# Weight casts in a fixed chain of two on GpSimd's queue, GpSimd's early arithmetic moved to VectorE

## The reference

```
h = rmsnorm(x, g_pre_mix[i])
layer 0: q,k,v,gate,mq = split(h @ w_in_ret)      # 6 heads of 128, retention in chunks of 128, rotary on q and k
         r = retention(q,k,v); self = groupnorm(r) * silu(gate)
layer 1: q,k,v,f,mq = split(h @ w_in_fox)         # 12 heads of 64, causal softmax with forget gates
mem = softmax(mq @ mk / 8) @ mv                   # 256 memory tokens, mk|mv = rmsnorm(mem) @ w_mem_kv
x = x + rmsnorm(concat(self, mem) @ w_out[i], g_post_mix[i])
h = rmsnorm(x, g_pre_mlp[i]);  u = relu(h @ w_up[i])
x = x + rmsnorm((u*u) @ w_down[i], g_post_mlp[i]) # 1024 -> 4096 -> 1024
```

## Time and profile before

| | us |
|---|---|
| median of three runs | 3964.7 |
| profiled execution | 3923.8 |
| its span, slowest core (3) | 3922.3 |
| spans of the 8 cores | 3885.5 to 3922.3 |
| TensorE busy | 3362.8 (86%) |
| VectorE / ScalarE / GpSimd busy | 1903.4 / 1722.5 / 458.3 |

### The profile page before, as it was taken

How to read it: one execution, slowest core, us unless ns; L and a number is a source line. 1 busy time by engine, 2 the same in 40 slices (tenths; PEclk the granted TensorE clock), 3 DMA queues, 4 the chain that set the end, 5 groups by cost and what they waited for, 6 DMA issues and landing times.

```text
span 3922.3 us, 56104 instructions; the slowest of 8 cores (3885.5 to 3922.3 us)
## 1 busy us (share of the span) xinstructions
PE 3362.8 (86%) x16476; PEld 1521.1 (39%) x16476; DVE 1903.4 (49%) x3201; ACT 1722.5 (44%) x3117; POOL 458.3 (12%) x422
## 2 busy tenths in 40 slices
PE   0536755699998999999999999999999999999997
PEld 0312322244443444444444444444444444444443
DVE  1435430346465654536246674565556664345252
ACT  0323310244734542574863443444734443755841
POOL 0111110001001220001011221010101210010010
PEclk9768877899999999999999999999999999999999
DMA  9779797744565554434435545445465454535334
GB/s 139 134 152 154 148 181 143 150 147 147 148 193 163 169 173 158 148 120 140 142 120 178 199 135 177 149 138 165 138 183 167 149 186 145 147 121 154 108 119 129
DMA packets 198262, 593.79 MB, mean 151 GB/s; under 512 B 49024, under 2 KB 60928, under 8 KB 196224
## 3 DMA queue, kind: packets, MB, share of 16 engines
q1 hardware_dynamic: 195296, 538.03, 45.0%
q0 software_dynamic: 2672, 52.17, 10.7%
HBM read 605.48 MB, written 88.87 MB: 177 GB/s over the span
## 4 chain that ended last, share of the span: by engine, by line
PE 66%; DMA 14%; DVE 8%; issue 4%; ACT 4%; another core or an unknown queue 2%; SPq 1%; POOL 1%; DVEq 0%; ACTq 0%; POOLq 0%
PE pb L598 66%; DMA wf_s<-wbf 6%; DMA xt_s<-xT 3%; DMA vcache<-un_s 2%; DVE un_s L618 2%; DVE tb_s L621 2%; DMA wm_s<-wbf 1%; SPq L633 1%; ACT rs_s L609 1%; ACT sq_s L609 1%; DVE hb_s L621 1%; POOL xt_s L618 1%; DMA mkv_s<-memkv 1%; DVE sq_s L618 1%
## 5 line engine op out<-in xcount | busy, mean ns | idle before, releaser
L598 PE MATMUL pb<-u_s,wf_s 128*128 128x512 bf16 x4096 | 987.4, 383 | 102.8 <-DMA wf_s<-wbf 73.7
L598 PE MATMUL pb<-hb_s,wf_s 128*128 128x512 bf16 x4096 | 968.4, 385 | 102.4 <-DMA wf_s<-wbf 75.9
L598 PE MATMUL pb<-hb_s,wm_s 128*128 128x512 bf16 (+1 forms) x2240 | 599.2, 387 | 56.0 <-DMA wm_s<-wbf 26.4
L598 PEld LDWEIGHTS pb<-hb_s,wf_s 128*128 128x128 bf16 x4096 | 396.3, 99 | 590.3 <-issue 161.1
L598 PEld LDWEIGHTS pb<-u_s,wf_s 128*128 128x128 bf16 x4096 | 398.4, 98 | 564.9 <-issue 133.8
L609 ACT ACTIVATE pt_s<-pb,dcol_s 128x512 bf16<-128x512 f32 x960 | 534.1, 628 | 71.2 <-PE pb L598 64.1
L609 ACT ACTIVATE rb_s<-pb 128x512 bf16<-128x512 f32 x512 | 304.4, 595 | 532.4 <-PE pb L598 456.8
L618 DVE TENSOR_TENSOR u_s<-rb_s 128x512 bf16<-128x512 bf16 x512 | 264.1, 516 | 497.5 <-ACT rb_s L609 496.1
L609 ACT ACTIVATE sq_s<-pb 128x512 bf16<-128x512 f32 x304 | 180.7, 596 | 712.2 <-DVE hb_s L630 678.0
L598 PE MATMUL pb<-un_s 65*128 65x512 bf16 (+5 forms) x1536 | 406.5, 305 | 12.5 <-DVE rs_s L618 4.2
L630 DVE CAST hb_s<-pb 128x512 bf16<-128x512 f32 x256 | 176.8, 691 | 452.1 <-PE pb L598 451.1
(11 more groups left out here) (65 smaller groups left out, 2403.9 us busy)
## 6 DMA issues: line engine op xcount, KB each, us to landing
wf_s<-wbf SPq DMA_DIRECT2D x512, 512.0 KB, 3.9
wm_s<-wbf SPq DMA_DIRECT2D x152, 768.0 KB, 4.8
xt_s<-xT SPq DMA_DIRECT2D x176, 256.0 KB, 6.4
wbf<-wall POOLq DMA_DIRECT2D x32, 1024.0 KB, 20.4
wm_s<-wbf SPq DMA_DIRECT2D x32, 512.0 KB, 4.2
outT<-xt_s SPq DMA_DIRECT2D x64, 256.0 KB, 2.7
wbf<-wall POOLq DMA_DIRECT2D x19, 768.0 KB, 18.1
vcache<-un_s SPq DMA_DIRECT2D x64, 144.0 KB, 4.2
```

What stands on the lines that cost most here:

```text
L598: S.add("pe", lambda e: e.matmul(out, lhsT=lhsT, rhs=rhs, start=start, stop=stop, **kw), reads=reads, writes=writes, cost=c)
```

## The change

The number of casts in flight goes from a modelled three to two that the hardware enforces: each cast names the cast two places before it as something it reads, so GpSimd waits for that cast's landing before it issues; the first two places before have none, and those casts name the fifth tile of x instead. The condition on TensorE's modelled time is gone, so all casts are recorded at the start of GpSimd's list. The cast's source and destination are written as rows of 1024 numbers (4 KB in f32) where they were 128 rows. For the first two blocks of the first sequence the elementwise operations that ran on GpSimd go to VectorE (`spare`), and `fox_prep` clears its tiles there always.

```diff
-NCAST = 3
+NCAST = 2
...
+    def rows(ap, o, n):
+        return ap[o * 131072:(o + n) * 131072].rearrange("(r f) -> r f", f=1024)
...
             r_ = gR[keys[0]]
-            if i >= NCAST:
-                p_ = rs_[i - NCAST]
-                yield lambda: S.avail["pe"] >= p_.last_w.end - 3000.0
-            yield ("pool", [], [])
-            S.add("pool", (... e.dma_start(out=d_, in_=s_).then_inc(sem, 16))(flat(DR["wbf"], o, n), flat(DR["wall"], o, n)),
-                  writes=[r_], dma=True, ncast=n)
+            after = [rs_[i - NCAST]] if i >= NCAST else [X[items[0]]["x"][4].R]
+            yield ("pool", after, [])
+            S.add("pool", (... e.dma_start(out=d_, in_=s_).then_inc(sem, 16))(rows(DR["wbf"], o, n), rows(DR["wall"], o, n)),
+                  reads=after, writes=[r_], dma=True, ncast=n)
...
+    def spare(s, b):
+        return "dve" if s == 0 and b < 2 else "pool"
...
-            tt(xs[c].ap, xs[c].ap, t.ap, ALU.add, ..., eng=("pool" if c % 2 else "dve"))
+            tt(xs[c].ap, xs[c].ap, t.ap, ALU.add, ..., eng=(spare(s, b) if c % 2 else "dve"))
...
-            tt(dst.ap, t1.ap, swp.ap, ALU.add, [t1.R, swp.R], [dst.R], eng="pool")
+            tt(dst.ap, t1.ap, swp.ap, ALU.add, [t1.R, swp.R], [dst.R], eng=e_)
...
-            tt(mix[:, h, :], rs.ap, sg.ap, ALU.mult, [rs.R, sg.R], [mixR[h]], eng="pool")
+            tt(mix[:, h, :], rs.ap, sg.ap, ALU.mult, [rs.R, sg.R], [mixR[h]], eng=spare(s, b))
...
-            memset(t.ap[:, :, 1, :], 1.0, [], [t.R], eng="pool")
+            memset(t.ap[:, :, 1, :], 1.0, [], [t.R])
```

More of the change, by code:

```diff
@@ L543, in caster @@
             r_ = gR[keys[0]]
-            if i >= NCAST:
-                p_ = rs_[i - NCAST]
-                yield lambda: S.avail["pe"] >= p_.last_w.end - 3000.0
-            yield ("pool", [], [])
-            S.add("pool", (lambda d_, s_: lambda e, sem: e.dma_start(out=d_, in_=s_).then_inc(sem, 16))(flat(DR["wbf"], o, n), flat(DR["wall"], o, n)),
-                  writes=[r_], dma=True, ncast=n)
+            after = [rs_[i - NCAST]] if i >= NCAST else [X[items[0]]["x"][4].R]
+            yield ("pool", after, [])
+            S.add("pool", (lambda d_, s_: lambda e, sem: e.dma_start(out=d_, in_=s_).then_inc(sem, 16))(rows(DR["wbf"], o, n), rows(DR["wall"], o, n)),
+                  reads=after, writes=[r_], dma=True, ncast=n)
             rs_.append(r_)
@@ L759, in seam @@
             stt(t.ap, hb.ap[:, c, :], gcol(gi, l, c), rs.ap, ALU.mult, ALU.mult, [hb.R[c], rs.R, cstR], [t.R])
-            tt(xs[c].ap, xs[c].ap, t.ap, ALU.add, [xs[c].R, t.R], [xs[c].R], eng=("pool" if c % 2 else "dve"))
+            tt(xs[c].ap, xs[c].ap, t.ap, ALU.add, [xs[c].R, t.R], [xs[c].R], eng=(spare(s, b) if c % 2 else "dve"))
             t.busy = False
@@ L1070, in rest @@
             bk.busy = False
-            yield ("pool", [t1.R, swp.R], [dst.R])
-            tt(dst.ap, t1.ap, swp.ap, ALU.add, [t1.R, swp.R], [dst.R], eng="pool")
+            e_ = spare(s, b)
+            yield (e_, [t1.R, swp.R], [dst.R])
+            tt(dst.ap, t1.ap, swp.ap, ALU.add, [t1.R, swp.R], [dst.R], eng=e_)
             if b == 0:
                 f0 = (qf0 if name == "q" else kf0)[hs.ap]
-                tt(f0.ap, t1.ap[:, 0:128], swp.ap[:, 0:128], ALU.add, [t1.R, swp.R], [f0.R], eng="pool")
+                tt(f0.ap, t1.ap[:, 0:128], swp.ap[:, 0:128], ALU.add, [t1.R, swp.R], [f0.R], eng=e_)
             t1.busy = False
@@ L1357, in fin @@
             act(r.ap, r.ap, AF.Exp, [r.R], [r.R], scale=-1.0)
-            tt(mix[:, p, :], o_.ap, r.ap, ALU.mult, [o_.R, r.R], [mixR[p]], eng="pool")
+            tt(mix[:, p, :], o_.ap, r.ap, ALU.mult, [o_.R, r.R], [mixR[p]], eng=spare(s, b))
             r.busy = o_.busy = False
```

## The result

The changed kernel took 4064.6 us (median of 4 runs, 4051.7 to 4082.6) where the kernel before took 3905.3 and 3928.0: ratio 1.038, 95% interval 1.029 to 1.048. Its other two runs, 3964.7 and 3985.1, fell into a slower state that some runs of most kernels here fall into, and no ratio counts such runs. The forecast was 3970 us and no change; the time lies just above its range and on the other side of 2%.

The account below looks back on a forecast made before the run. Prediction: DMA engines alternate between cast pieces and load rows, so an unbroken cast queue starves TensorE. 514 us until casts end + 3411 remaining work + 15 restart = 3940 us span; 3970 us with the runs' median allowance, range 3860 to 4060.

Parts of the forecast that it names:

- late stretch: TensorE from 800 us on, untouched by the change: 3122.3 us for 2926.6 us of work, used as a rate of 1.067.
- End of casting: GpSimd's casts from about 12 us without pause: 52.17 MB at 104 GB/s take 502 us, ending at 514 us.
- The rest at 1.067: TensorE's work left after the casts, 3196.8 us, at 1.067 us each: 3411 us.
- The allowance for mixing parts alone, 15 us: Right after the casts only mixing parts without an MLP beside them can run: 15 us, between nothing and 34.
- The 30 us from span to time: Median of the runs lies 41 us above the profiled execution; two thirds of that turn 3940 into 3970 us.
- Rows of 4 KB: Casts written as 4 KB rows come out as the same transfer with pieces as large as before: cost zero.
- First cast and x: At the start, first cast piece at 12 us, x tiles in by some 15 us instead of 87.86.
- Reissue: On GpSimd, issuing a cast after a landing takes a few us, under 10, so two in flight leave no pause.
- 18.6 loads: While casts run, a load costs 9 of 167 turns, so 18.6 loads pass, allowing at most 47 us of TensorE work.
- Arithmetic at zero: Moving the first blocks' arithmetic to VectorE, about 70 us there, fits its idle time: cost zero, at most 30 us.
- Loads pass freely: Rival during casting: loads get through between cast pieces or in pauses, span 3806 us; chance 0.16 together with faster casts, 3800.
- The starved start: Rival at the start: casts delay positions and memory tokens, about 25 us of work done by 541 us, span 4009; chance 0.23.

Follow-up runs that it names:

- The three sizes of piece: The changed kernel with casts in pieces of 32 KB (the change itself), 8 KB and 2 KB written: 4065, 4000 and 3882 us.
- the short rows: The changed kernel with each cast cut into rows of 4 KB read and 2 KB written that cannot be joined: 3882 us, 0.993 against the kernel before.

## Why the prediction failed

The mechanism it named is the one at work: turns of a cast piece and a load's row, a cast queue that is never empty, TensorE starved until the casts end. The three sizes of piece, one cast in flight against two and four, and the arithmetic put back show it. The forecast of no change failed because four terms of the sum were too small. By the weight loads of the earlier trace rows, one matmul of the late stretch takes 3122.3 / 14579 = 0.2142 us.

- *End of casting.* Forecast 514 us, measured 533.6: 52.17 MB in 520 us are 100 GB/s where I took 104. **+20 us.**
- *The rest at 1.067.* I measured work as busy time times the mean clock of its stretch, 3196.8 us left. By matmuls 16143 are left at 534 us, x 0.2142 = 3457 us, where the forecast has 3411. **+46 us.** The mean clock of a stretch takes in the waits, in which it is low, as two pieces of the kernel before show, one of waiting and one of work:

```profile
586.00:614.00 28.00, 0.00 (x0) 0.00 (x0) 0.00 (x0) 0.00 (x0) 0.00 (x0) 0.57 0.99 123
649.00:679.00 30.00, 30.00 (x141) 13.62 (x140) 4.47 (x8) 2.39 (x4) 0.00 (x0) 1.00 0.51 156
```

  Work of the early stretch was thus counted at 0.78 where much of it ran at 1.00, and the idle time to be recovered looked larger than it was.
- *The allowance for mixing parts alone, 15 us.* From 534 to 800 us 998 matmuls take 266 us where the late rate gives 214: **52 us, +37 more than allowed**, and beyond the 34 I had as its upper end. The first 66 us hold most of it:

```profile
534.00:600.00 66.00, 35.52 (x143) 14.71 (x147) 45.73 (x94) 26.16 (x54) 0.00 (x0) 0.62 0.33 112
```

  147 matmuls, worth 31 us at the late rate, with the clock at 0.62, VectorE busy for 45.73 us, and TensorE waiting for it and for ScalarE: 35 us lost. TensorE is busy 76% of the time until 800 us, where I had above 90%. I had priced the restart as low occupancy at full clock. How much of it is the clock and how much the chain through VectorE (with the moved arithmetic on it) was not tried apart.
- *The late stretch.* 15145 matmuls in 3250 us, **+7 us** over the rate of before.

3940 + 20 + 46 + 37 + 7 = 4050, the span measured. Early and late matmuls differ in size, so how the last three terms divide is rough; their sum is not: from 534 us on 3516 us were measured where the forecast had 3411 + 15. The 30 us from span to time, taken from a median of 3964.7, were not borne out either: the changed kernel's median lies 15 us above its span.

The other steps. *Rows of 4 KB:* right, 2672 packets as before; the short rows only worked once they could not be merged. *First cast and x:* right (13.4 us, x by 16), and its limit too, as the run with this part alone shows. *Reissue:* right for two in flight. *18.6 loads:* wrong in its count, and right in the work done partly by luck. 5822 packets passed, some 40 loads. Those on the prediction's list had landed by 369 us, five heads among them; of those issued behind, 17 were x tiles and positions of the next block and only three were `wf` loads, the first of which landed at 538.7 us. So twice as many loads gave TensorE 52 us of work (21.66 x 0.88 + 59.62 x 0.55) where I had 47. *Arithmetic at zero:* wrong by some 14 us by itself. The large price of that move is another: it empties GpSimd's list, and with the list the pauses. The prediction said so of the kernel before (GpSimd's arithmetic made the pauses) but never priced them as a part of the change. Single edits now do, each against the kernel before: the wait for x 0.992, with the chain of two 0.998, with the arithmetic moved 1.038. That is about -30, +20 (the two intervals overlap a little) and +160 us. The second step also drops the condition on TensorE's modelled time; the two were not tried apart. The third price hangs on the chain: with one cast in flight the same move costs some 40 us (3824 against 3783).

The rivals. *Loads pass freely* is refuted for this change: from 13 to 534 us no kind of load has a median under 29 us. By the rule of the Trainium skill, "DMA: Bandwidth & Descriptors", section "Queues, rings and completion order", a turn should be 9 to 17 descriptors. That is enough for a whole load, and since a cast of 1024 KB has three packets on each engine (48 in all), a load or more would pass with each cast. In the 130 us above thirteen casts were moved and, at 144 packets each, 4.3 loads; 624 to 624, and 2.2 to 1 over all of the casting, say otherwise. *The starved start* gave about the right time (4009 us of span) by a way that did not happen: it wanted casts after 535 us with under 30 us of work, and there were 52. Its other half, the mixing parts' full price, did happen, and more (52 us where it had 34).

## What to carry to other kernels

Before moving work off an engine that also issues a background transfer, ask what that work did to the transfer's pace: the waits in its list may be what lets the urgent loads through. A bulk transfer whose results are needed over a longer time did best here with one cast in flight and gaps, not as fast as it could go; look at the packets of both queues, and at the order of the urgent loads, to see who gets through. When a starved stretch is priced, count what is left in instructions at the late rate, and add what the restart loses.

## What the runs showed of the hardware

- Two queues shared the engines one packet for one packet, 624 and 624 in 130 us, so a queue of 24 and 32 KB pieces took 92.2% of the time. Over all of the casting with two casts in flight it was 2.2 rows to a piece, with one in flight 9.6, with four 1.4.
- A tensor cut into contiguous rows of 4 KB was moved in the same 2672 packets as one of large rows; set apart, the rows made 26399.
- The casts' engine time was 7140 us with two in flight and 5720 with one, for the same bytes.
- TensorE's clock stood at 0.55 while it was starved (85 to 534 us), 0.62 in the 66 us after, and 0.99 from 800 us on. In the kernel before it was 0.57 in 28 us without a matmul and 1.00 in 30 us full of them.
